# First mixer's opening: loads in pieces, operands split without the root, root applied at read-out, squares on GpSimd and ScalarE, forget tiles over four banks

## What is computed

```python
h = concatenate([meta, x], axis=1)                 # 16 + 256 = 272 tokens
hn = x * rsqrt(mean(x * x, axis=-1) + 1e-6) * g    # rmsnorm over 1024 features
q, f_pre, i, g = split(hn @ w_in, 4, axis=-1)      # w_in: 1024 x 4096
f = lb + (1.0 - lb) * sigmoid(f_pre)
logf, k = log(f), 1.0 - f
# then, for each of 8 heads, the chunkwise recurrence
# S_t = diag(f_t) S_{t-1} + k_t v_t^T,  o_t = S_t^T q_t
```

## Time and profile before

| | us |
|---|---|
| median of three runs | 1578.69 |
| the three runs | 1577.25, 1578.69, 1581.88 |
| the profiled execution | 1577.86 |
| its span | 1576.1 |
| busy in the span: PE, DVE, ACT, POOL | 1458.9, 1042.8, 780.3, 282.8 |

### The profile page before, as it was taken

One profiled execution on the slowest core, in us unless ns is written; L12 is line 12 of the kernel. 1 busy time (PEld: TensorE's weight loads), 2 busy tenths in 40 slices (PEclk: granted clock), 3 DMA queues, 4 the chain that ended last, 5 costly groups with the idle time before them and its releaser, 6 DMA issues. The chain is left out here.

```text
span 1576.1 us, 29025 instructions
## 1 busy us (share of the span) xinstructions
PE 1458.9 (93%) x11301; PEld 1397.5 (89%) x11301; DVE 1042.8 (66%) x1727; ACT 780.3 (50%) x1272; POOL 282.8 (18%) x384
## 2 busy tenths in 40 slices
PE   5999879999787997999988899989999988999997
PEld 4999769999787876999987789989999987899997
DVE  5664678877775546788877755357877675587643
ACT  5654644544355544555535555565343554544341
POOL 0000102220054420122001143102332100122210
PEclk9999999999998998999998999999999998999999
DMA  7432525659522213565872311136775733275451
GB/s 279 177 128 107 189 98 221 225 172 346 204 107 107 81 55 107 193 237 208 323 280 73 116 54 55 64 124 222 280 254 207 240 113 134 107 277 211 146 177 45
DMA packets 41140, 265.80 MB, mean 169 GB/s; under 512 B 4560, under 2 KB 5712, under 8 KB 15440
## 3 DMA queue, kind: packets, MB, share of 16 engines
q1 hardware_dynamic: 41040, 264.44, 46.6%
HBM read 263.38 MB, written 1.05 MB: 168 GB/s over the span
## 5 line engine op out<-in xcount | busy, mean ns | idle before, releaser
L224 DVE TENSOR_TENSOR w_lo<-raw,w_hi 128x2048 fp32r<-128x2048 f32 (+2 forms) x207 | 426.3, 2064 | 215.0 <-ACT w_hi L220 211.2
L220 ACT ACTIVATE w_hi<-raw 128x2048 fp32r<-128x2048 f32 (+3 forms) x224 | 385.9, 1727 | 37.8 <-PE bank L414 33.7
L412 PE MATMUL bank<-x_hi_up,w_hi 128*128 128x272 f32 (+1 forms) x704 | 203.7, 289 | 8.3 <-DVE x_lo_up L717 8.1
L414 PE MATMUL bank<-x_hi_up,w_lo 128*128 128x272 f32 (+1 forms) x704 | 201.8, 287 | 0.0
L413 PE MATMUL bank<-x_lo_up,w_hi 128*128 128x272 f32 (+1 forms) x704 | 201.4, 286 | 0.0
L412 PE MATMUL bank<-z_hi,w_hi 128*128 128x258 f32 x704 | 200.5, 285 | 0.0
L413 PE MATMUL bank<-z_lo,w_hi 128*128 128x258 f32 x704 | 198.9, 283 | 0.0
L414 PE MATMUL bank<-z_hi,w_lo 128*128 128x258 f32 x704 | 198.2, 282 | 0.0
L412 PEld LDWEIGHTS bank<-x_hi_up,w_hi 128*128 128x128 f32 x704 | 133.4, 190 | 10.3 <-issue 8.8
L413 PEld LDWEIGHTS bank<-x_lo_up,w_hi 128*128 128x128 f32 x704 | 133.9, 190 | 0.0
L413 PEld LDWEIGHTS bank<-z_lo,w_hi 128*128 128x128 f32 x704 | 133.4, 190 | 0.1
(11 more groups left out here) (461 smaller groups left out, 3888.0 us busy)
## 6 DMA issues: line engine op xcount, KB each, us to landing
raw<-w_up SPq DMA_DIRECT2D x44, 1024.0 KB, 4.8
raw<-w_gu SPq DMA_DIRECT2D x44, 1024.0 KB, 4.8
work<-w_ada SPq DMA_DIRECT2D x27, 1024.0 KB, 5.1
raw<-w_down SPq DMA_DIRECT2D x32, 704.0 KB, 5.6
raw<-w_dn SPq DMA_DIRECT2D x32, 704.0 KB, 4.1
raw<-w_a_in SPq DMA_DIRECT2D x16, 1024.0 KB, 5.5
mod_w_down<-w_ada SPq DMA_DIRECT2D x16, 1024.0 KB, 6.0
raw<-w_gdn_qkv SPq DMA_DIRECT2D x12, 1024.0 KB, 4.8
```

Source lines behind the costliest of these rows:

```text
L220: act.activation(w_hi[:, s, 0:blocks * P], raw[:, s, 0:blocks * P], ACT.Copy).then_inc(hi_split.sem, 1)
L224: dve.tensor_tensor(w_lo[:, s, 0:blocks * P], raw[:, s, 0:blocks * P], w_hi[:, s, 0:blocks * P].bitcast(F32), ALU.subtract).then_inc(lo_sp ...
L412: pe.matmul(o, w_hi[:, s, b], x_hi[:, xk, cols[0]:cols[1]], start=begin, stop=False)
L414: last = pe.matmul(o, w_lo[:, s, b], x_hi[:, xk, cols[0]:cols[1]], start=False, stop=end)
```

## The change

The first block goes. Everything is issued and awaited in the mixer's block.

- Loads: parameters first; h in four quarters with a semaphore each, the first half of item 0 between the first and second; the second half; items 1 to 3; the constants in two parts, without `ones`; `c_row`; then the ring as before. POOL writes `ones` itself.
- Operand split: ACT rounds h times gain directly to `x_hi`, DVE makes `x_lo` from h, gain and `x_hi`. `rstd` is not in it.
- Squares: POOL multiplies blocks 0 to 3 and adds them pairwise (two sums), ACT squares blocks 4 to 7. PE sums these six with `ones` after the first tile (`add_up`).
- Item 0 is split in halves. The first tile waits for the first half, the second for the rest. Item 1 follows; ACT's items 2 and 3 come behind the root, DVE's items 2 to 7 behind single f tiles.
- Read-out: DVE multiplies every tile by `rstd` on its way from the bank. Sigmoid and Silu are done by ACT in place afterwards; f and k of tile n - 1 are made by DVE behind the read-out of tile n.
- The eight f tiles use banks 0 to 3, and a tile waits for the one four before it; later tiles use banks 0 and 1 as before.
- One-element activations with Exp and with Sqrt load those tables early.

```diff
-                sp.dma_start(h[:, :, :], hT_d).then_inc(h_in.sem, 16)
-                sp.dma_start(params[:, :], params_d).then_inc(params_in.sem, 16)
-                sp.dma_start(consts[:, :], consts_d[:, 0:NHELD]).then_inc(consts_in.sem, 16)
...
+                def bank_of(event):
+                    return bank[turn[event] % (4 if turn[event] < KD else 2)]
...
+                    sp.dma_start(params[:, :], params_d).then_inc(params_in.sem, 16)
+                    source, at = SOURCE[A_ITEMS[0]]
+                    for i in range(4):
+                        sp.dma_start(h[:, 2 * i:2 * i + 2, :], hT_d[:, 2 * i:2 * i + 2, :]).then_inc(h_in[i], 16)
+                        if i == 0:
+                            sp.dma_start(raw[:, 0, 0:half_item], w[source][at, :, 0:half_item]).then_inc(open_in.sem, 16)
+                    sp.dma_start(raw[:, 0, half_item:ITEM], w[source][at, :, half_item:ITEM]).then_inc(raw_loaded[0], 16)
+                    for r in range(1, SLOTS):
+                        load(sp, A_ITEMS[r], r, r % SLOTS)
+                    sp.dma_start(consts[:, 0:P], consts_d[:, 0:P]).then_inc(consts_in.sem, 16)
+                    sp.dma_start(consts[:, 2 * P:NHELD], consts_d[:, 2 * P:NHELD]).then_inc(consts_in.sem, 16)
+                    sp.dma_start(c_row[:, :], c_d).then_inc(c_in.sem, 16)
...
-                        if t == 0:
+                        if m == 0:
+                            pe.wait_ge(open_lo.sem, open_lo.at(1))
+                        elif t == 0 or m == 1:
                             pe.wait_ge(lo_split.sem, r + 1)
-                        if m >= 2:
+                        if m >= KD:
                             tile_taken(pe, in_turn[m - 2])
+                        elif m >= 4:
+                            tile_taken(pe, in_turn[m - 4])
...
+                    def add_up():
+                        pe.wait_ge(pairs_added.sem, pairs_added.at(1))
+                        parts = [0, 1, 4, 5, 6, 7]
+                        for k_ in parts:
+                            if k_ >= 4:
+                                pe.wait_ge(late_squared.sem, late_squared.at(k_ - 3))
+                            last = pe.matmul(bank[6][:, 0:T1], ones, work[:, k_, :], start=k_ == 0, stop=k_ == KD - 1)
...
+                    for k_ in range(2):
+                        low_part(k_)
+                    dve.wait_ge(open_hi.sem, open_hi.at(1))
+                    dve.tensor_tensor(w_lo[:, 0, 0:half_item], raw[:, 0, 0:half_item], w_hi[:, 0, 0:half_item].bitcast(F32),
+                                      ALU.subtract).then_inc(open_lo.sem, 1)
+                    for k_ in range(2, KD):
+                        low_part(k_)
...
+                        if kind == "tile":
+                            tile_ready(dve, event)
+                            dve.tensor_tensor({"q": q, "f": f, "v": v, "g": g}[part][:, n, :],
+                                              bank_of(event)[:, 0:T1], rstd[:, :], ALU.mult).then_inc(copied_out.sem, 1)
+                            if part == "f" and n:
+                                keys(n - 1)
+                        r = None
                         if kind == "tile" and part == "f":
+                            r = {0: 2, 2: 3, 3: 4, 4: 5, 5: 6, 7: 7}.get(n)
+                        elif kind == "tile" and n % 2 and ring_of(event) < final:
                             r = ring_of(event) + SLOTS
+                        if r is not None:
                             split_lo(dve, r, r % SLOTS, 0, item_of(r)[3])
...
+                    for k_ in range(2, KD):
+                        high_part(k_)
+                    for k_ in range(KD // 2, KD):
+                        act.activation(work[:, k_, :], h[:, k_, :], ACT.Square).then_inc(late_squared.sem, 1)
...
+                    act.activation(mod_sum[:, 0, 0:1], eps_col[:, 0:1], ACT.Sqrt)
+                    act.wait_ge(sum_made.sem, sum_made.at(1))
...
+                            if part == "f" or part == "g" and n >= 4:
+                                tile_taken(act, event)
+                                d = (f if part == "f" else g)[:, n, :]
+                                done = gated if part == "f" else silued
+                                act.activation(d, d, ACT.Sigmoid if part == "f" else ACT.Silu).then_inc(done.sem, 1)
...
+                    for k_ in range(KD // 2):
+                        if k_ % 2 == 0:
+                            pool.wait_ge(h_in[k_ // 2], 16)
+                        pool.tensor_tensor(work[:, k_, :], h[:, k_, :], h[:, k_, :], ALU.mult).then_inc(squared.sem, 1)
+                    pool.wait_ge(squared.sem, squared.at(KD // 2))
+                    pool.tensor_tensor(work[:, 0:2, :], work[:, 0:2, :], work[:, 2:4, :], ALU.add).then_inc(pairs_added.sem, 1)
```

More of the change, by code:

```diff
@@ L823, in fused_model @@
         eps_col = sbuf(ctx, "eps_col", [P, 1])
-        h_in, params_in, consts_in, c_in = sig("h_in"), sig("params_in"), sig("consts_in"), sig("c_in")
+        params_in, consts_in, c_in = sig("params_in"), sig("consts_in"), sig("c_in")
+        h_in = [ctx.enter_context(nc.semaphore(f"h_in{i}")) for i in range(4)]
         c_ready = sig("c_ready")
-        with nc.Block() as block:
-            @block.sync
-            def _(sp):
-                sp.dma_start(h[:, :, :], hT_d).then_inc(h_in.sem, 16)
-                sp.dma_start(params[:, :], params_d).then_inc(params_in.sem, 16)
-                sp.dma_start(consts[:, :], consts_d[:, 0:NHELD]).then_inc(consts_in.sem, 16)
[L834 to L849, removed]
         def modulation_scales(parts):
@@ L1142, in tensor @@
                             product_tile(event)
+                            if event == in_turn[0]:
+                                add_up()
                         elif event[0] == "head":
@@ L1198, in head, with low_part, keys @@
                                               ALU.subtract).then_inc(diffed.sem, 1)
+                    def low_part(k_):
+                        dve.wait_ge(x_high.sem, x_high.at(k_ + 1))
+                        dve.scalar_tensor_tensor(x_lo[:, k_, :], h[:, k_, :], gain(k_), x_hi[:, k_, :].bitcast(F32), ALU.mult,
+                                                 ALU.subtract).then_inc(x_split.sem, 1)
+                    def keys(n):
+                        dve.wait_ge(gated.sem, gated.at(n + 1))
+                        dve.tensor_scalar(f[:, n, :], f[:, n, :], lb[:, 5, n:n + 1], lb[:, 4, n:n + 1], ALU.mult,
+                                          ALU.add).then_inc(f_made.sem, 1)
+                        dve.wait_ge(f_made.sem, f_made.at(n + 1))
+                        dve.tensor_scalar(k[:, n, :], f[:, n, :], -1.0, 1.0, ALU.mult, ALU.add).then_inc(k_made.sem, 1)
+                    dve.memset(eps_col[:, :], EPS).then_inc(eps_set.sem, 1)
                     dve.wait_ge(params_in.sem, 16)
@@ new lines, in vector @@
+                    dve.wait_ge(hi_split.sem, 1)
+                    dve.wait_ge(open_lo.sem, open_lo.at(1))
+                    dve.tensor_tensor(w_lo[:, 0, half_item:ITEM], raw[:, 0, half_item:ITEM],
+                                      w_hi[:, 0, half_item:ITEM].bitcast(F32), ALU.subtract).then_inc(lo_split.sem, 1)
+                    split_lo(dve, 1, 1, 0, 16)
+                    dve.wait_ge(std_made.sem, std_made.at(1))
+                    dve.reciprocal(rstd[:, :], std[:, :]).then_inc(rstd_made.sem, 1)
@@ L1224, in vector @@
-                        if kind == "tile" and n % 2 and ring_of(event) < final:
+                        if kind == "tile":
[5 more added lines that the diff above has]
+                        r = None
@@ L1270, in scalar @@
                         if kind == "tile":
-                            o = bank[turn[event] % 2][:, 0:T1]
-                            tile_ready(act, event)
-                            dst = {"q": q, "f": f, "v": v, "g": g}[part]
-                            func = ACT.Sigmoid if part == "f" else ACT.Silu if part == "g" and n >= 4 else ACT.Copy
-                            act.activation(dst[:, n, :], o, func).then_inc(copied_out.sem, 1)
                             if n % 2 and ring_of(event) < final:
```

63 lines of the change are left out of this document (38 added, 25 removed).

## The result

The changed kernel takes 1568.68 us (median of 4 executions, 1562.21 to 1569.76) against 1579.72 (4 executions, 1577.25 to 1581.88): a ratio of 0.9923 with the interval 0.9898 to 0.9948. Two more series gave 1565.82 against 1577.09 (0.9921, 0.9895 to 0.9946) and 1567.57 against 1578.70 (0.9932, 0.9917 to 0.9947). The ratios are formed from all executions; the quotients of the medians are 0.9930, 0.9929 and 0.9929. Faster, then, by 0.7 to 0.8%, some 11 us.

What follows compares the result with a forecast made beforehand. PE was taken as the bound, with time lost only where it stands or runs slowly in the opening. Start, first tile, sum, seven f tiles and stalls put the first head at 56.15 against 71.83: 1577.86 - 15.7 = 1562.2 us, range 1559 to 1568.

Steps and rivals of the forecast that it cites:

- the head steps: PE's steps of about 9.85 us behind the opening: two read-outs add 0.75 on DVE, claimed to cost nothing.
- rival D: Eight full head steps: DVE's read-outs stall PE in each, making the kernel slower, 1583.8 us; chance 0.03.
- PE starts at 8.5: Opening: first weight product at 8.5 us against 21.47, bounds 8.2 to 9.5.
- Rival C: Opening loads: pieces do not land early, PE starts near 11.4, 2.9 us lost, 1565.1 us; chance 0.06.
- 0.3 added: Opening: 0.3 us added to PE's start because GpSimd's multiplications and DVE's low split disturb each other.
- The port pair: Opening: GpSimd and DVE hold the shared SBUF ports in turn; six low parts up to 2.3 us later, about 13.
- The first tile takes 4.95: First f tile on PE: 4.3 us at half rate, then full rate, 4.95 us in all, ending at 13.45.
- DVE is late next: f tiles to first head: DVE has 24.0 us of work plus idle; PE stalls 0.5 and 0.25 us.
- Keys(1): DVE's pair of steps making f and k of tile 1: waits about 1.5 us for ACT's sigmoid behind item 4's split.
- rival A: f tiles: DVE becomes the bound; at 3 us more slip, 1565.2 us; chance 0.18.
- keys(0): DVE's steps making f and k of tile 0: wait some 0.5 us for ACT's sigmoid; by the skill page 1.4 later.
- The anchor: PE's first head, behind the sixth q and v tile: 56.15 against 71.83, 15.7 us earlier, all gained in the span.

Runs made afterwards that it cites:

- short parameters: Changed kernel with only the first 128 parameter columns loaded ahead of h: median 1567.25, ratio 0.9925; with the sigmoids of f1 and f3 moved too, 1560.59, 0.9897.

## Why the prediction came out as it did

**Right:** the mechanism and the sign. The stand of 3.1 us and the stretch at 0.50 went, the sum of squares took 2.91 us (2.95 said) and lies behind the tile, all seven other f tiles run gapless at full rate, and the head steps cost nothing (so no rival D: the lead is 12.8 at the first head and still 13.0 at 199.57, behind all of them). The head came at 59.06, not 56.15. The 2.9 us between are 2.16 for PE's start, 0.77 for the first tile, 0.4 back because f1 starts 2.55 us behind the start of the sum and not 2.95, and 0.4 between f1 and the head.

**"PE starts at 8.5": 10.66.** The first of the two mis-sized terms, 2.16 us. Parameters and first quarter of h came as said (3.64 and 4.54 against 3.8 and 4.5), but the first half item landed at 8.04 instead of 5.8. The constant rate of 411 KB/us failed (columns of the earlier trace rows; the kernel before, the changed kernel, then the one with h whole):

```profile
3.00:5.00 2.00, 0.00 (x0) 0.00 (x0) 0.00 (x0) 0.00 (x0) 0.00 (x0) 1.00 1.01 422
5.00:7.00 2.00, 0.00 (x0) 0.00 (x0) 0.00 (x0) 0.00 (x0) 0.00 (x0) 1.00 1.00 402
```

```profile
3.00:5.00 2.00, 0.00 (x0) 0.00 (x0) 0.98 (x6) 0.65 (x3) 0.46 (x1) 1.00 0.95 303
5.00:7.00 2.00, 0.00 (x0) 0.00 (x0) 1.69 (x4) 0.50 (x2) 0.78 (x2) 1.00 0.91 225
9.00:11.00 2.00, 0.34 (x1) 0.37 (x2) 1.87 (x2) 2.00 (x6) 2.00 (x2) 1.00 1.05 435
```

```profile
3.00:5.00 2.00, 0.00 (x0) 0.00 (x0) 0.89 (x6) 0.21 (x1) 0.00 (x0) 1.00 1.07 433
5.00:7.00 2.00, 0.00 (x0) 0.00 (x0) 0.23 (x2) 0.20 (x1) 0.22 (x1) 1.00 0.89 279
```

So the rate was right for the kernel before, and did not carry over to the new order of loads. Rival C named the late landing, but its start (11.4) was too late for each profile of the changed kernel (9.45 to 10.66), and a rate shared among transfers is not its cause alone, since the sum over all transfers was low itself. In the first profile the half split then took 1.43, near the "0.3 added".

**The port pair.** The sentence drawn from the Trainium skill, "SBUF — State Buffer" (Who interferes with whom, on the shared port pair), put the end of the six low parts up to 2.3 us late, and the sum did without it. They took 4.04 us instead of 2.56, 1.5 us late, and end at 14.5, not near 11 (the other 2 us are the late start). The trace agrees with the page in kind; PE's slow first tile covered all but some 0.3 us of it.

**"The first tile takes 4.95": 5.72.** Half rate lasted to 16.1, 5.4 us behind the first product, not 4.3. In the second profile it ended at 13.45, 3.1 us behind it. The tile took 4.66 and 4.93 us in the other two profiles, so the term is right as a mean; its spread of 1.1 us passes to f1's start.

**"DVE is late next": in the right place, too cheaply.** Keys(1) waited 1.02 us in the first profile and 1.94, 2.26, 2.59 where PE started earlier. The rule that the experiments bear out is the later of two: f1's start plus 39.9 to 40.1 us of PE's work, or VectorE's chain through keys(1), 58.3 to 59.1 (61.75 in the execution in which item 4 came latest). This is rival A, at 2.2 to 3 us. With the 2.16 us late start PE's own work decided; starts of 9.45 and 9.93 left the head at 58.3 and 58.8 all the same. From the predicted f1 start of 16.4 PE's own work would have led to 56.4, but VectorE's chain came out at 58.3 or later in every profile that it decided, so a start at 8.5 alone would not have given 56.15. In the second and third profile PE stands 1.01 and 1.35 us ahead of q0, which the prediction had named as a sign of being wrong. The four banks, called needed, are worth half a microsecond at the head in the one profile without them, within the 0.7 us by which the changed kernel's own heads scatter.

**"ScalarE: Activation LUTs".** By this page of the Trainium skill (What ACT_TABLE_LOAD costs) keys(0) would come 1.4 us later. It waited 0.48, and the sigmoid starts 1.29 us after its table's load (23.44 to 24.73): the trace disagrees with the drain once more.

**Behind the mixer.** "Stretches behind the first mixer change by over 1 us" was named as what would make it wrong, and one did: 1.4 us from 1305 to 1333, 2.9 in all behind the first head in the profiled execution. The sum took what is gained at the head as gained in the span, with PE's rate behind the mixer as given. It is not: the same kernel takes 1561.5 to 1569.8 us, and its median over 16 executions lies 5.8 us above its best. The anchor fell 2.9 us short (12.8 for 15.7), the rest of this execution gave 2.9, and so 1562.2 met 1562.21 by luck. At the medians of the three series the gain is 11.0 to 11.3 us and by the ratios 10.7 to 12.5, somewhat less than the 12.8 to 13.5 of the three heads, though in two of the three series the interval leaves room for all of it. The kernel before with its block dissolved shows outside its interval that a lead at the head need not arrive.

## What to carry to other kernels

Take a gain at an anchor just behind the edit, and the remaining span apart: here the anchor held to 0.8 us over three profiles of one kernel while the span moved by 7.1. Do not count the lead at the anchor as time won until the ratio of many executions shows it: 3.6 us at the head of the kernel with its block dissolved came to nothing clear of noise. Where an engine's queue mixes work that waits for a transfer with a short step that another engine needs, put the short step first: moving two sigmoids took a wait of 1 to 2.6 us away, and with the short parameters gave the earliest head (57.75). And an earlier start is worth nothing beyond what the next chain allows; look for that chain's waits before paying for the start.

## What was not expected of the hardware

A stretch of transfers runs slowly without being the first and whatever its row length. In the changed kernel the rates are 248, 186, 264 and 315 GB/s in the four microseconds from 4 to 8 us, and 421 in the next; rows of 4096 bytes take 216 to 266 ns on the mean of each of these microseconds and 159 later, and rows of 8192 bytes in their place are slow too (322 to 414 ns, 309 later). It is not that a program's first transfers are slow: the kernel before moves 422 GB/s from 3 to 5 us, with its block dissolved 418, and with h whole it is 433; there the rate falls to 238 and 221 only from 6 to 8 us, when the half item is fetched. In the kernel before item 0 comes behind the constants and runs at 429 from 8 to 9 us. So the slow stretch goes with item 0 being fetched in the first 8 us; what makes it slow is open.

PE ran its first tile at 0.227 us a matmul with the granted clock shown as 1.00 (10 to 19 us), so that column doesn't tell of the slow beginning; the spacing of the matmuls does. And an execution of one and the same kernel has its PE at the lower level in stretches that others run at full rate (0.77 against 1.00 from 560 to 575 us). One such stretch comes whole or not at all, at 3.05 to 3.10 us each time, and the 16 executions of the changed kernel spread over 8.3 us.
